# One of four weight sums in three groups of a fast matrix product is made by an adding transfer

## What is computed

```
h2 = rms_norm(x, g_ffn)
return x + jnp.square(jax.nn.relu(h2 @ w_up)) @ w_down
```

## Time and profile before

| | |
|---|---|
| median of 3 runs | 995.33 us (995.07 to 996.58) |
| profiled execution, its own time | 995.78 us |
| span of the profiled execution | 994.0 us |
| TensorE busy | 977.5 us, 98% of the span |
| VectorE busy | 599.1 us, 60% of the span |
| GpSimd busy | 30.2 us, 3% of the span |
| granted TensorE clock, mean | 0.998 of full |

### The profile page before, as it was taken

The page is one execution under the profiler, slowest core; times in us unless marked ns, Lnnn a source line. Parts: engine busy times, 40 slices in busy tenths (PEclk is TensorE's granted clock), DMA queues, the critical chain, the costliest instruction groups (busy, mean ns, idle before and its releaser), DMA issues.

```text
span 994.0 us, 12120 instructions
## 1 busy us (share of the span) xinstructions
PE 977.5 (98%) x4932; PEld 595.2 (60%) x4932; DVE 599.1 (60%) x1166; ACT 217.7 (22%) x429; POOL 30.2 (3%) x40
## 2 busy tenths in 40 slices
PE   6999999999999999999999999999999999999998
PEld 4944445755555448999744478458744444568443
DVE  5766941245677887866898772998957651341211
ACT  4313312213241123422100021001103212353000
POOL 3000000000001600000000000000000000000000
PEclk9999999999999999999999999999999999999999
DMA  9451731434235534344444444242334334211721
GB/s 311 155 191 47 271 127 43 166 112 146 85 113 187 162 114 176 121 170 170 170 169 169 170 170 169 86 169 86 125 130 170 122 132 169 85 43 44 253 85 42
DMA packets 59543, 139.73 MB, mean 141 GB/s; under 512 B 2864, under 2 KB 6208, under 8 KB 59488
## 3 DMA queue, kind: packets, MB, share of 16 engines
q1 hardware_dynamic: 57568, 134.56, 38.8%
q0 software_dynamic: 1712, 4.32, 1.9%
q10 hardware_dynamic: 208, 0.08, 0.0%
HBM read 137.90 MB, written 1.05 MB: 140 GB/s over the span
## 4 chain that ended last, share of the span: by engine, by line
PE 93%; DVE 5%; ACT 2%; issue 0%; ACTq 0%; DVEq 0%
PE pair L1719 54%; PE pair L1802 13%; PE pair L2038 6%; PE pair L1806 4%; PE turned L1660 4%; PE score L2038 3%; DVE arena L852 2%; PE turned L2038 1%; PE score L2189 1%; PE score L2133 1%; PE score L2202 1%; PE score L1886 1%; PE score L1935 1%; PE score L1885 1%; PE score L1951 1%; PE turned L2120 0%
## 5 line engine op out<-in xcount | busy, mean ns | idle before, releaser
L1719 PE MATMUL pair<-ring,hT 128*128 128x512 f32 (+2 forms) x896 | 385.6, 584 | 0.0
L1719 PEld LDWEIGHTS pair<-ring,hT 128*128 128x128 f32 x896 | 166.9, 191 | 183.7 <-issue 179.6
L852 DVE TENSOR_TENSOR arena<-arena 128x256 f32<-128x256 f32 (+9 forms) x304 | 186.9, 630 | 23.7 <-ACT arena L518 11.2
L1719 PE MATMUL pair<-ring,arena 128*128 128x512 f32 (+1 forms) x224 | 90.6, 562 | 0.0
L1092 DVE CUSTOM_DVE_ANT_0 arena<-score,masks 128x256 f32<-128x256 f32 (+2 forms) x40 | 18.1, 451 | 105.2 <-PE score L1886 46.6
L1719 PE MATMUL pair<-hT,ring 128*128 128x128 f32 (+2 forms) x464 | 76.4, 324 | 0.2 <-ACT hT L557 0.2
L1719 PEld LDWEIGHTS pair<-hT,ring 128*128 128x128 f32 (+1 forms) x464 | 66.0, 188 | 9.0 <-issue 1.3
L1719 PEld LDWEIGHTS pair<-ring,arena 128*128 128x128 f32 x224 | 42.1, 190 | 44.3 <-issue 43.5
L528 ACT ACTIVATE arena<-turned 128x512 f32<-128x512 f32 (+2 forms) x66 | 32.7, 536 | 136.5 <-PE turned L1660 136.5
L1660 PEld LDWEIGHTS turned<-ident,arena 128*128 128x128 f32 (+1 forms) x363 | 42.9, 146 | 27.1 <-issue 15.2
L852 DVE TENSOR_TENSOR arena<-pair,arena 128x512 f32<-128x512 f32 x41 | 28.3, 691 | 50.2 <-PE pair L1719 37.2
(11 more groups left out here) (214 smaller groups left out, 889.8 us busy)
## 6 DMA issues: line engine op xcount, KB each, us to landing
ring<-in_w_in SPq DMA_DIRECT2D x33, 2048.0 KB, 8.4
ring<-in_w_up SPq DMA_DIRECT2D x8, 2048.0 KB, 8.6
ring<-in_w_down SPq DMA_DIRECT2D x8, 2048.0 KB, 7.7
ring<-in_w_o SPq DMA_DIRECT2D x4, 2048.0 KB, 8.6
ring<-in_w_mem_kv SPq DMA_DIRECT2D x2, 2048.0 KB, 7.8
ring<-in_w_glu SPq DMA_DIRECT2D x2, 2048.0 KB, 8.2
ring<-in_w_ssm_out SPq DMA_DIRECT2D x2, 2048.0 KB, 7.8
ring<-in_w_ukv SPq DMA_DIRECT2D x4, 512.0 KB, 3.9
```

The costliest lines, as they stand in the source:

```text
L852: return dve.tensor_tensor(o, a, b, op)
L1719: ins = pe.matmul(o_, s, m, start=a, stop=b)
```

## The change

For groups 4, 5 and 6 (`ADDED`) VectorE no longer makes T3. GpSimd waits until T1 of the group is made, so that b12 in the slot isn't read any more, and then issues a transfer from w_up in DRAM that adds b22 onto b12 where it lies in the slot: 128 partitions x 4 x 512 numbers, 1 MB. Product 7 reads T3 from the slot, and waits for the semaphore `added` instead of `group_sums`. The counts of `group_sums` after it are one lower, which `sums_at` works out. The wait for the y weights, which stood ahead of T3, now stands ahead of T2.

```diff
+ADDED = range(UP + 1, UP + 4)
...
+def sums_at(i, n):
+
+    left_out = sum(j in ADDED for j in range(i)) + (i in ADDED and n > 2)
+    return 4 * i + n - left_out
...
+            if i in ADDED:
+                t3 = b12
...
+            for i in ADDED:
+                pool.wait_ge(sem("group_sums"), sums_at(i, 1))
+                c0 = JOBS[JOB[f"g{i}y"]][5]
+                pool.dma_start(group(i)[4][1], d["w_up"][0, 512:DM, c0 + 512:c0 + DM].rearrange("(k p) n -> p k n", p=P),
+                               accum_op=ALU.add).then_inc(sem("added"), 16)
...
             def group_t2(i):
 
                 _, _, (_, _, _, b22), _, (t2, _) = group(i)
+                weights_in(f"g{i}y")
                 dve.wait_ge(sem("group_product"), product_at(i, 5))
...
             for i in range(UP, UP + 4):
-                if i > UP:
-                    group_t3(i)
                 group_t2(i)
...
                 def summed(n):
-                    pe.wait_ge(sem("group_sums"), 4 * i + n)
+                    if n == 2 and i in ADDED:
+                        pe.wait_ge(sem("added"), 16 * (i - ADDED[0] + 1))
+                    else:
+                        pe.wait_ge(sem("group_sums"), sums_at(i, n))
```

More of the change, by code:

```diff
@@ L168 @@
     "group_product": "TensorE: products of the groups of seven, in order", "group_act": "ScalarE: Q1 and Q5 copied, first block out",
-    "group_rows": "sums of a group's rows", "group_sums": "sums of a group's weights: T1, T3, T2, T4",
+    "group_rows": "sums of a group's rows", "group_sums": "sums of a group's weights: T1, T3, T2, T4; T3 is left out where GpSimd's transfer adds",
+    "added": "a group's T3, added by its transfer",
     "second_out": "blocks made of sums alone", "group_z": "Q5 less Q7 out of PSUM", "first_out": "Q6 and the second block out of PSUM", "last_out": "the third block out of PSUM",
```

## The result

The changed kernel takes **1003.33 us** (median of 4 runs, 1002.39 to 1006.52), against 995.32 us for the kernel before (995.07 to 996.58). The ratio is 1.0083, with a 95% interval of 1.0058 to 1.0109: slower by 8.0 us. The prediction was 1000.4 us, in a range of 994.8 to 1011.0 us, with a chance of 0.62 for slower.

The account below looks back on a forecast made before the run. The prediction took TensorE alone to bound the stage, with VectorE's removed sums worth nothing. Waits of 2.0 us in group 5 and 3.1 us in group 6 made 5.1 us on 995.33: 1000.4 us, range 994.8 to 1011 us.

Parts of the forecast that it names:

- What bounds the kernel: Up projection: TensorE alone bounds it, so removing 6.87 us of VectorE sums gains nothing, at most 1.3 us.
- The cost of the transfer: Groups 4 to 6: 2.8 us fixed plus 5.8 us data, 8.6 us alone; ends 5.8 us after the load would have landed.
- The loads beside the transfer: Sign in the profile after: loads sharing the DMA engines in groups 4 to 6 take 11 to 14 us instead of 8.5.
- The three moments of use: Product 7 of groups 4, 5 and 6 leaves the transfer 14.6, 11.3 and 9.6 us from release to landing.
- The sum of 5.1 us: Product 7's waits of 2.0 us in group 5 and 3.1 us in group 6 add up; group 4 doesn't wait.
- The 1.2 us that this load was to cost: Group 6: late `down0` delays T4 and so product 4, costing 1.2 us only if product 7 didn't wait.
- are later by as much: Groups 5 and 6: products behind product 7 are delayed by exactly its waits, 2.0 and 3.1 us, with nothing given back.
- the forecast's own range: Whole kernel if groups 5 and 6 wait 2 to 8 us in all: 997.3 to 1003.3 us, chance 0.42.
- the transfers that get in each other's way: Rival, groups 4 to 6: landing after 18.0 us, waits of 18.5 us together, 1013.8 us; over 8 us slower, chance 0.20.
- The hidden transfer: Rival, groups 4 to 6: adding costs as much as copying, landing after 8.6 us, no waits, 995.3 us; chance 0.34.
- The upper bound of 18.0 us: Adding transfer's landing if each of four 256 KB parts cost 3.8 us beside a load, plus 2.8 us fixed.
- Worth for VectorE's freed time: Rival: TensorE's waits behind T3 shrink, at most 1.3 us, 994.0 us; chance of over 2 us faster 0.04.

Follow-up runs that it names:

- the plain copy: Changed kernel with GpSimd's transfer copying b22 over b12 without adding, all else as in the changed kernel: 996.85 us, ratio 1.0011.
- group 6 alone: Changed kernel with the adding transfer only in group 6, groups 4 and 5 making T3 on VectorE as before: 1000.87 us, ratio 1.0046.
- the load held back: Changed kernel with SyncE issuing the x loads of groups 5 and 6 only after the previous group's adding transfer landed: 1001.47 us, ratio 1.0063.
- three quarters: Changed kernel with the adding transfer cut to three of its four parts (768 KB): 1000.48 us, ratio 1.0047.
- the last kernel: Changed kernel with T3 of groups 4 to 6 made by nobody, product 7 using b12 and waiting for no sum: 995.57 us, ratio 1.0001.

## Why the prediction was right, and where it was short

*What bounds the kernel: right.* TensorE's waits in the stage were not for VectorE. The kernel without the sums takes 0.1 us more than the kernel before, with an interval of about 1 us to each side: the removed 6.9 us of VectorE are worth nothing that can be told.

*The cost of the transfer: right, from a row of another kind.* The sum took the data part of a 2 MB load for the 1 MB that is added: 8.6 us alone, and a landing at 5.8 us past that of the load beside it. Alone it landed after 8.5 and 8.7 us. Beside the load, in the changed kernel, T1 of group 6 ended at 465.22 us (462.93 + 2.29) and the transfer landed at 478.3 us (465.68 + 12.6), 13.1 us later, where 12.6 us was worked out; in group 5 it was 13.5 us, where 13.3 us was. Of the fixed part some was hidden in a place that the rows had not shown: the issue stands 0.5 us behind T1, and an issue that adds takes 1.3 us where the copy takes 0.8. The rule of the Trainium skill in "Collectives: The Full Stack", that a reduction runs at half the rate of a copy because it reads twice, agrees with the traces: 215 GB/s against some 400 with the engines full in both cases. That the second read is the reason is the account of the Trainium skill; the runs show the rate, and that it goes with the adding, since the plain copy of the same shape is faster. The formula of the Trainium skill in "DMA: Bandwidth & Descriptors", by which 4.4 us for 1 MB is an estimate, is a good deal under all that was seen: 8.5 us for the adding transfer alone, and 9.7 us and more for the plain copy beside a load. A plain 1 MB copy of GpSimd with nothing beside it was not run. The loads beside the transfer were less late than forecast, 10.2 to 10.8 us from issue to landing instead of 11 to 14.

*The three moments of use: right.* Group 4 had 14.6 us and did not wait. Group 5 was to wait 2.0 us and waited 2.16; group 6 was to wait 3.1 us and waited 3.39. The sum of 5.1 us was 5.55 us. That the waits add up, and that the late load of `down0` costs nothing beside a late product 7, held too. The 1.2 us that this load was to cost without such a wait was misread from the rows: T4 of group 6 starts behind 0.78 us of idle time, which takes up that much of a delay of 2.2 us, so T4 would end at 482.8 us and product 4 would be 0.4 us late. The sum doesn't use this term.

*The step that failed* is the sentence that products 3, 6 and 4 and all behind them "are later by as much". They were later by more. A term was missing from the sum: behind each of the two waits TensorE worked for some 3.4 us at 1.2 GHz, 1.63 and 1.73 us, 3.4 us together. The measured 8.0 us are 5.5 us of waiting and most of this. Why not all of it, the mean clocks of the executions suggest. Traces with one fallen stretch have a mean of 0.998 (the kernel before, group 6 alone, the load held back), those with two 0.996 (the changed kernel, three quarters), and those with none 1.000. Two of the four executions of the changed kernel took 1002.4 and 1002.5 us with a mean of 0.998, and an estimate with one stretch gives 995.3 + 5.55 + 1.7 = 1002.5 us; the profiled one took 1004.2 us with 0.996, and with two stretches the sum is 1004.2 us. The fourth took 1006.5 us with 0.995, more than this accounts for, and has no trace. So the clock seems to have fallen behind both waits in some executions and behind one of them in others, as it did in some traces and not in others behind the 1.5 us at 122 us, and the median lies between two cases. What decides it no run here shows.

The measured time is 2.9 us over the predicted one and at the very end of the forecast's own range (1003.3 us). It was well inside the stated range only because that range was wide on this side for another reason, the transfers that get in each other's way. This part was luck.

*The rivals.* The hidden transfer fell: a landing of 9.6 us after T1 was needed in group 6, and even the plain copy took 10.6 us from its issue. The upper bound of 18.0 us was far too high. It came from a transfer that read one row 128 times, and a transfer that shares the engines with a load delayed that load by 2.4 us here and not by 4.4. Worth for VectorE's freed time fell with the last kernel.

## What to carry to other kernels

Before work is moved off an engine, ask whether the engine that bounds the kernel waits for it: a kernel that leaves that work out puts the ceiling on all ways of moving it in one run. Price an adding transfer as twice its bytes, add the load that will run beside it to the full, and compare the landing with the moment of use, place by place; where it is late, a later moment of use (product 7 behind product 3) costs less than a faster transfer. And price a new wait of TensorE above its own length when it is of some 2 us: behind such waits the products ran at half the clock for 3.4 us in every trace here, though not in every execution, as far as the mean clocks tell. Before two profiles are subtracted, look for such stretches in both: here the kernel before had one of its own, worth 1.55 us.

## What the runs showed of the hardware

- With waits of 2.16, 2.53, 3.39, 3.88 and 4.05 us in the up projection TensorE was granted 0.50 of its clock for 3.4 us, from between 0.6 us before it resumed (the wait of 3.88 us) and 1.3 us after (that of 2.53 us), at a cost of 1.4 to 1.7 us each time. After waits of 0.49 and 1.18 us it kept the full clock, and so it did when spare products filled waits of 2.2 and 3.4 us. After the wait of 1.5 us at 122 us, the same in all ten traces, the clock fell in two of them, at a cost of about 1.5 us where it could be read, and not in eight.
- An adding transfer of float32 from DRAM onto SBUF, issued by GpSimd, kept the DMA engines full at 210 to 215 GB/s. 1 MB lands 8.5 us after its issue alone, and 12.6 to 13.2 us beside a 2 MB load, which lands 2.1 to 3.0 us late.
- An issue of 128x4x512 numbers takes GpSimd 0.75 to 0.81 us as a copy and 1.27 to 1.41 us when it adds.
